# MLA attention one head at a time, with values and ones as the stationary operand of the value products

## The chip, the cores and the metric
One NeuronCore of a Trainium2 chip runs the whole kernel in one launch. The metric is the device time of that core in microseconds (us). Each core has TensorE (PE, matrix products; the loads of its stationary operand are listed as PEld), VectorE (DVE), ScalarE (ACT), GpSimd (POOL) and SyncE (SP, which issues most DMAs). The engines run their own instruction streams in order and wait for each other through semaphores.

## The reference
Two layers of a streaming encoder run for a prompt of 512 new frames and a sample of 32 new frames with 256 cached ones; both share the weights. The part that matters here is branch B of the token mixer, multi-head latent attention (MLA) with 8 heads, keys of 96 features and values of 64:

```python
def attend_mla(q, q_pos, k, v, k_pos):
    s = jnp.einsum('bqhd,bkhd->bhqk', q, k).astype(jnp.float32) * (MLA_QK ** -0.5)
    mask = (k_pos[None, :] // CHUNK) <= (q_pos[:, None] // CHUNK)
    s = jnp.where(mask[None, None], s, -jnp.inf)
    w = jax.nn.softmax(s, axis=-1).astype(v.dtype)
    return jnp.einsum('bhqk,bkhd->bqhd', w, v)
```

CHUNK is 64, so a tile of 128 queries sees all keys up to its own end, and its first 64 queries don't see the last 64 keys. The output of the 8 heads (512 features for each frame) is multiplied by w_br_mla and merged with the two other branches under sigmoid gates.

## The kernel before, in words
In each of the two layers the work comes in stages: entry and projections, keys and queries (kq), stick-breaking attention (the L941 to L971 products), MLA attention, the gated branch products (the loop `branches`), the output projection, the routing and the experts. All MLA operands are f32.

The 544 frames are five tiles: t = 0 to 3 are 128 prompt frames each, t = 4 is the 32 sample frames. MLA runs 40 units, a unit being one tile of queries and one head. `MLA_ORDER = [3, 2, 1, 0, 4]` (L65) puts all 8 heads of tile 3 first (512 keys), then those of tile 2 (384), 1 (256), 0 (128), and the sample's 8 units last (288 keys). For unit n:
- PE `scores(n)`: queries stationary, 128*(t+1) keys moving, into PSUM bank n % 3; for the prompt a one-row product (L1006) adds the mask.
- DVE `neg_max(n)`: the negated maximum of each query's row.
- ACT L1480: the exponential out of PSUM into `pr`, with that maximum as bias; `accum_out` gives the row's sum in `sums` (a second instruction in the trace).
- PE `turn(n)`: transposes of the weights, 128 keys at a time, into bank 3 or 4.
- DVE L1858: copy of the turned weights into `pt` (two buffers).
- PE `values(n)`: for each 128 keys the turned weights [128 keys x 128 queries] are stationary and 64 value columns of the head move; the output [queries x 64] of all heads of the tile lies side by side in bank 5 or 6.

When a tile's 8 heads are done, DVE `normalise` takes the reciprocals of the sums and multiplies the 512 columns, PE `turn_out` (L1051) transposes them in four pieces into bank 7, and ACT `out_rows` (L1472) copies them into `ybr`, which has features on partitions.

PE's order is written out by hand: scores(n+2), values(n-1), turn(n), and two units after a tile's end its turn_out. So the scores run two units ahead. ACT and DVE also split f32 operands of the branch stage into a rounded high part and a low remainder: `high(j)` on ACT (L1443) and `low(j)` on DVE after units 5, 10, 14, 18 and 22, a gate weight after unit 26 (`gate_high`, `gate_low`, 1024 columns), and the remaining eight after the stage. Behind the last unit PE issues filler products, `busy(0, 1)` (L760; the identity times 512 constant columns, read by nobody), turns the last output, and waits for ACT's copy (semaphore o_ev) before `branches`. GpSimd has no part in the stage. `x_ybr[:, 2:6]`, where MLA's output goes, is unused until then; `vv` holds the values of 7 key tiles, 512 columns each. In the kq stage a DVE copy (L1789) fills `vv` for each key tile.

## Time and profile before

| | us |
|---|---|
| median of 3 runs | 1545.51 |
| lowest and highest | 1540.42 and 1546.64 |
| the profiled execution's own time | 1546.93 |
| its span in the trace | 1545.2 |
| mean granted TensorE clock | 0.958 |
| PE busy | 1418.6 (92%) |
| DVE busy | 766.5 (50%) |
| ACT busy | 623.4 (40%) |
| MLA stage, layer 0, first scores to first branch product | 225.06 to 299.21 |

Times inside the trace count from the start of the span. A busy time counts instructions of that engine, and matmuls overlap in it, so that the start of the next instruction says more of a matmul's cost than its length. PEclk is the granted TensorE clock as a share of the full 2.4 GHz.

### The profile page before, as it was taken

The page shows a single profiled execution, that of the slowest core. Times are in us where ns is not written, and L with a number is a line of the kernel's source. Part 1 is how long each engine was busy: PE and PEld are TensorE (multiplying, and loading weights), DVE is VectorE, ACT ScalarE, POOL GpSimd, SP SyncE. Part 2 cuts the span into 40 slices and gives each one's busy share as a digit, 9 for nine tenths or more (in the row PEclk, how much of TensorE's full clock was granted, in tenths as well). Part 3 has the DMA queues.
Part 4 walks back from the last instruction along what each step waited for, and adds up shares of the span by engine and source line. Part 5 has one row for each costly group of instructions (what it writes and reads, how often), then busy time and mean ns, then how long its engine had stood idle before and what let it go on. Part 6 is the DMA issues. An engine that isn't in the chain of part 4 may idle for free.

```text
span 1545.2 us, 21380 instructions
## 1 busy us (share of the span) xinstructions
PE 1418.6 (92%) x8610; PEld 1142.6 (74%) x8610; DVE 766.5 (50%) x1121; ACT 623.4 (40%) x966; POOL 111.2 (7%) x128
## 2 busy tenths in 40 slices
PE   5998999999999988999479999999999999899991
PEld 5995657699999756777279846577999988567760
DVE  4326316534335346887353282265433353578863
ACT  4317634422224144656243285244222241456550
POOL 0300010000000011000203001000000000110002
PEclk9999899899999999999879998998999999999996
DMA  7222300032224456998722102000332263589955
GB/s 259 69 73 97 109 0 1 1 110 71 64 82 172 197 209 236 400 413 309 243 105 69 60 12 98 0 1 1 109 102 68 76 227 127 208 332 418 409 201 201
DMA packets 95928, 229.52 MB, mean 149 GB/s; under 512 B 14410, under 2 KB 64612, under 8 KB 82916
## 3 DMA queue, kind: packets, MB, share of 16 engines
q1 hardware_dynamic: 83252, 179.58, 32.1%
q0 software_dynamic: 7360, 29.89, 5.5%
q10 hardware_dynamic: 5232, 18.88, 3.0%
q8 instruction: 58, 0.95, 0.2%
q14 instruction: 26, 0.21, 0.0%
HBM read 197.69 MB, written 34.84 MB: 150 GB/s over the span
## 4 chain that ended last, share of the span: by engine, by line
PE 86%; DMA 4%; DVE 4%; ACT 3%; issue 2%; POOL 1%; ACTq 0%; POOLq 0%; SPq 0%; DVEq 0%
PE ps L775 10%; PE ps L777 9%; PE ps L776 9%; PE ps L1215 7%; PE ps L1195 3%; PE ps L1194 3%; PE ps L1193 3%; PE ps L941 3%; PE ps L1036 3%; PE ps L801 2%; PE ps L1101 2%; PE ps L1103 2%; PE ps L1102 2%; PE ps L803 2%; PE ps L802 2%; PE ps L760 2%
## 5 line engine op out<-in xcount | busy, mean ns | idle before, releaser
L1672 DVE TENSOR_TENSOR work<-work,ps 128x544 f32<-128x544 f32 x48 | 34.6, 721 | 213.0 <-ACT work L1526 213.0
L1526 ACT ACTIVATE work<-ps 128x544 f32<-128x544 f32 x48 | 30.0, 625 | 249.0 <-PE ps L777 249.0
L776 PE MATMUL ps<-xn_r,ksv_r 128*128 128x272 f32 x384 | 112.9, 294 | 0.0
L776 PE MATMUL ps<-xn_r,work_r 128*128 128x272 f32 x384 | 110.7, 288 | 0.0
L720 POOL DMA_INDIRECT rows_back<-xrow_d,row_of x32 | 38.2, 1193 | 951.5 <-DVE row_of L2001 735.2
L1195 PE MATMUL ps<-ew_r,rows_tok_r 128*128 128x512 f32 x256 | 100.1, 391 | 0.0
L802 PE MATMUL ps<-wr_r,qt_ht_r 128*128 128x256 f32 (+1 forms) x320 | 93.4, 292 | 0.0
L801 PE MATMUL ps<-work_r,qt_ht_r 128*128 128x256 f32 x240 | 72.8, 303 | 14.0 <-DVE rows_lo_r L1672 7.9
L1672 DVE TENSOR_TENSOR ew_r<-ew,gu_hi_a_r 128x2048 fp32r<-128x2048 f32 x32 | 73.1, 2291 | 17.1 <-ACT gu_hi_a_r L1547 17.1
L776 PEld LDWEIGHTS ps<-xn_r,ksv_r 128*128 128x128 f32 x384 | 74.4, 194 | 0.0
L776 PEld LDWEIGHTS ps<-xn_r,work_r 128*128 128x128 f32 x384 | 72.1, 188 | 0.0
L803 PE MATMUL ps<-work_r,rows_lo_r 128*128 128x256 f32 x240 | 71.5, 298 | 0.0
L1480 ACT ACTIVATE work<-ps,nmax 128x512 f32<-128x512 f32 (+4 forms) x80 | 41.6, 519 | 60.0 <-DVE nmax L1837 59.8
L802 PEld LDWEIGHTS ps<-wr_r,qt_ht_r 128*128 128x128 f32 x320 | 65.1, 204 | 0.0
L1837 DVE TENSOR_REDUCE nmax<-ps 128x1 f32<-128x512 f32 (+4 forms) x80 | 38.4, 480 | 53.1 <-PE ps L1006 46.4
L1547 ACT ACTIVATE gu_hi_a_r<-ew 128x2048 fp32r<-128x2048 f32 x32 | 60.7, 1908 | 5.9 <-ACT yo_b L1587 5.9
L760 PE MATMUL ps<-con 128*128 128x512 f32 x92 | 59.3, 782 | 4.0 <-ACT work L1461 4.0
L1102 PE MATMUL ps<-wr_r,qt_ht_r 128*128 128x512 f32 (+1 forms) x160 | 62.7, 392 | 0.0
L801 PEld LDWEIGHTS ps<-work_r,qt_ht_r 128*128 128x128 f32 x240 | 49.9, 208 | 15.4 <-DVE rows_lo_r L1672 9.0
L1672 DVE TENSOR_TENSOR wr_r<-wr,work_r 128x2048 fp32r<-128x2048 f32 x10 | 25.7, 2572 | 70.0 <-ACT work_r L1300 70.0
L1215 PE MATMUL ps<-ew,acts 128*128 128x512 f32 x128 | 58.8, 602 | 1.1 <-issue 1.1
L1215 PE MATMUL ps<-ew,act_b 128*128 128x512 f32 x128 | 57.7, 594 | 1.1 <-issue 1.1
(344 smaller groups left out, 4047.8 us busy)
## 6 DMA issues: line engine op xcount, KB each, us to landing
wr<-in_w_in SPq DMA_DIRECT2D x68, 512.0 KB, 4.7
ew<-in_w_exp_gate SPq DMA_DIRECT2D x32, 1024.0 KB, 7.1
ew<-in_w_exp_up SPq DMA_DIRECT2D x32, 1024.0 KB, 10.8
ew<-in_w_exp_down SPq DMA_DIRECT2D x32, 1024.0 KB, 9.9
wr<-in_w_out SPq DMA_DIRECT2D x16, 512.0 KB, 4.3
rows_d<-yo_a ACTq DMA_DIRECT2D x16, 512.0 KB, 8.2
rows_d<-yo_b ACTq DMA_DIRECT2D x16, 512.0 KB, 8.4
xres_d<-x_keep SPq DMA_DIRECT2D x2, 2048.0 KB, 7.0
```

Source lines behind the costliest of these rows:

```text
L760: mm(bank(b), ident, con[:, 0:512], start=True, stop=True, skip_group_check=True)
L775: mm(out_[h], w_hi, x_hi[:, c], start=first, stop=False, skip_group_check=True)
L776: mm(out_[h], w_hi, x_lo[:, c], start=False, stop=False, skip_group_check=True)
L777: ins = mm(out_[h], w_lo, x_hi[:, c], start=False, stop=last, skip_group_check=True)
L801: mm(bank(g % 6, n), hi_, w_hi[:, k, :], start=(k == 0), stop=False)
L802: mm(bank(g % 6, n), hi_, w_lo[:, k, :], start=False, stop=False)
L803: ins = mm(bank(g % 6, n), lo_, w_hi[:, k, :], start=False, stop=(k == DC - 1))
L1102: mm(bank(b, 512, TM[t]), hi_, wo_low[h][k], start=False, stop=False, skip_group_check=True)
L1195: ins = mm(bank(2 + s), xg_hi[s][:, k, :], low, start=False, stop=(k == DC - 1))
L1215: ins = mm(bank(4 + 2 * s + a), ehT[s][:, P * k:P * k + P], down_w[i][:, k, 512 * a:512 * a + 512], start=(k == 0), stop=(k == 1))
L1547: f(gu_high[s][h], gu_w[i][:, :, 4 * h:4 * h + 4, :].rearrange("p m k n -> p k m n"), ACT.Copy).then_inc(gu_up[0], 1)
L1672: return v_.tensor_tensor(o_, a, b, op)
```

## The change
The units are put in another order (MLA_UNITS): first the sample's 8 heads, then for each head its prompt tiles 3, 2, 1, 0. The value product is turned round: the stationary side is [128 keys x 128 columns], 64 value columns of the head beside 64 ones, and the moving side is up to 512 queries of turned weights. Its output has 64 partitions of features and 64 partitions that all hold the sum of the weights. A head's prompt tiles are collected in `pt` (now two buffers of 4 key blocks x 512 queries), and `values(h)` runs four products for the whole head, of 512, 384, 256 and 128 columns, into bank 6 or 7. The sample's outputs go to bank 5 (`sample_values`).

The values are laid out in groups of 192 columns (even head, ones, odd head). The 7 key tiles don't fit in `vv` like this, so a part of them goes to x_ybr[:, 2:6], and GpSimd writes the ones in the kq stage. ACT's exponentials lose `accum_out`. ACT takes over the copy of tile 3's turned weights (`weights_out`) and computes reciprocals of the denominators as exp(-ln(sum)) over 512 columns on 64 partitions (`denominators`); DVE multiplies (`normalise`) straight into `ybr`. The transposes of the output, `turn_out`, and ACT's `out_rows` are gone. `busy(0, 1)` becomes `busy(0, 2)`.

```diff
@@ -62,14 +62,14 @@
 SBC = 1376
 NEG = -1e30
-MLA_ORDER = [3, 2, 1, 0, 4]
+MLA_UNITS = [(h, 4) for h in range(HEADS)] + [(h, t) for h in range(HEADS) for t in (3, 2, 1, 0)]
...
         aa = work[:, 2 * SBC:4 * SBC].rearrange("p (s n) -> p s n", s=2)
         pr = work[:, 0:1536].rearrange("p (s n) -> p s n", s=3)
-        pt = work[:, 1536:2560].rearrange("p (s n) -> p s n", s=2)
-        ot = work[:, 2560:3072]
+        pt = work[:, 1536:5632].rearrange("p (s j n) -> p s j n", s=2, j=4)
+        pt_s = work[:, 5632:5824].rearrange("p (s n) -> p s n", s=2)
+        rden = work[:, 5824:6336]
...
                  + [big_r[:, (8 + i) * T:(9 + i) * T] for i in range(4)])
+        vv_a, vv_b = vv[:, :, :].rearrange("p t n -> p (t n)"), x_ybr[:, 2:6, :].rearrange("p k n -> p (k n)")
+        VP = 192
+        vv_pairs = [vv_a[:, 4 * VP * j:4 * VP * j + 4 * VP] for j in range(4)] + [None] + [vv_b[:, 4 * VP * j:4 * VP * j + 4 * VP] for j in range(2)]
+        vv_split = [vv_a[:, 16 * VP:18 * VP], vv_b[:, 8 * VP:10 * VP]]
+        def thirds(ap):
...
-        pt_ev = sem("pt_ev", NU)
-        pv_mm = sem("pv_mm", NU)
-        o_nrm = sem("o_nrm", NTILE)
-        o_tr = sem("o_tr", NTILE)
-        o_ev = sem("o_ev", NTILE)
+        pt_ev = sem("pt_ev", NU - HEADS)
+        pt_act = sem("pt_act", HEADS)
+        pv_mm = sem("pv_mm", 2 * HEADS)
+        o_nrm = sem("o_nrm", HEADS + 1)
+        den = sem("den", 2 * HEADS + 4)
         pw_high = sem("pw_high", 6)
         pw_low = sem("pw_low", 6)
...
                     nc.gpsimd.tensor_tensor(xn[:, k, :], f32(rows_hi[:, k, :]), f32(rows_lo[:, k, :]), ALU.add).then_inc(xn_rdy[0], 1)
+                pool.wait_ge(cm_mm[0], at(cm_mm, l, 4))
+                pool.wait_ge(spill[0], at(spill, l, 16))
+                pool.wait_ge(xn_rdy[0], at(xn_rdy, l, DC))
+                stand(pool)
+                for rows_ in (vv_a[:, 0:18 * VP], vv_b[:, 0:10 * VP]):
+                    nc.gpsimd.memset(thirds(rows_)[:, :, 1, :], 1.0).then_inc(ones_in[0], 1)
                 if l == 0:
-                    pool.wait_ge(cm_mm[0], 4)
...
-                    t, h = MLA_ORDER[n // HEADS], n % HEADS
+                    h, t = MLA_UNITS[n]
                     if n >= 3:
                         pe.wait_ge(s_exp[0], at(s_exp, l, n - 2))
...
                 def turn(n):
-                    t = MLA_ORDER[n // HEADS]
+                    t = MLA_UNITS[n][1]
                     pe.wait_ge(s_exp[0], at(s_exp, l, n + 1))
-                    if n >= 2:
-                        pe.wait_ge(pt_ev[0], at(pt_ev, l, n - 1))
+                    if n >= 2 and MLA_UNITS[n - 2][1] == 3:
+                        pe.wait_ge(pt_act[0], at(pt_act, l, MLA_UNITS[n - 2][0] + 1))
+                    elif n >= 2:
...
-                def values(n):
-                    t, h = MLA_ORDER[n // HEADS], n % HEADS
-                    pe.wait_ge(pt_ev[0], at(pt_ev, l, n + 1))
-                    i = n // HEADS
-                    if h == 0 and i >= 2:
-                        pe.wait_ge(o_nrm[0], at(o_nrm, l, i - 1))
-                    dst = ps[0:TM[t], 5 + i % 2, 64 * h:64 * h + 64]
-                    if t < 4:
-                        for j in range(t + 1):
-                            ins = mm(dst, pt[:, n % 2, P * j:P * j + P], vv[:, j, 64 * h:64 * h + 64], start=(j == 0), stop=(j == t))
+                def key_rows(j, h, m=P):
+                    pair, lo = h // 2, VD * (h % 2)
+                    if j == 4:
+                        rows_ = vv_split[pair // 2][0:m, VP * (pair % 2):VP * (pair % 2) + VP]
                     else:
-                        for j in (1, 2):
-                            mm(dst, pt[:, n % 2, DEC * j:DEC * j + DEC], vv[:, 4 + j, 64 * h:64 * h + 64], start=(j == 1), stop=False)
-                        ins = mm(dst, pt[0:DEC, n % 2, 0:DEC], vv[0:DEC, 4, 64 * h:64 * h + 64], start=False, stop=True)
+                        rows_ = vv_pairs[j][0:m, VP * pair:VP * pair + VP]
+                    return rows_[:, lo:lo + P]
+                def sample_values(h):
+                    pe.wait_ge(pt_ev[0], at(pt_ev, l, h + 1))
+                    dst = bank(5, DEC, P, DEC * h)
+                    for j in (1, 2):
+                        mm(dst, key_rows(4 + j, h), pt_s[:, h % 2, DEC * j:DEC * j + DEC], start=(j == 1), stop=False, skip_group_check=True)
+                    ins = mm(dst, key_rows(4, h, DEC), pt_s[0:DEC, h % 2, 0:DEC], start=False, stop=True, skip_group_check=True)
                     ins.then_inc(pv_mm[0], 1)
-                def turn_out(i):
-                    t = MLA_ORDER[i]
-                    pe.wait_ge(o_nrm[0], at(o_nrm, l, i + 1))
-                    if i:
-                        pe.wait_ge(o_ev[0], at(o_ev, l, i))
-                    if t == 4:
-                        stand(pe)
+                def values(h):
+                    pe.wait_ge(pt_ev[0], at(pt_ev, l, HEADS + 3 * h + 3))
+                    pe.wait_ge(pt_act[0], at(pt_act, l, h + 1))
+                    if h >= 2:
+                        pe.wait_ge(o_nrm[0], at(o_nrm, l, h))
                     for j in range(4):
-                        ins = nc.tensor.transpose(bank(7, TM[t], P, P * j), ot[0:TM[t], P * j:P * j + P], ident[0:TM[t], 0:TM[t]])
-                    ins.then_inc(o_tr[0], 1)
+                        ins = mm(bank(6 + h % 2, SEQ - P * j, P, P * j), key_rows(j, h), pt[:, h % 2, j, P * j:SEQ], start=(j == 0), stop=(j == 3), skip_group_check=True)
+                    ins.then_inc(pv_mm[0], 1)
+                pe.wait_ge(ones_in[0], at(ones_in, l, 2))
                 scores(0)
                 scores(1)
                 for n in range(NU):
                     if n + 2 < NU:
                         scores(n + 2)
-                    if n >= 1:
-                        values(n - 1)
+                    if 1 <= n <= HEADS:
+                        sample_values(n - 1)
+                    if n > HEADS and n % 4 == 0:
+                        values(n // 4 - 3)
                     turn(n)
-                    if n % HEADS == 2 and n > HEADS:
-                        turn_out(n // HEADS - 1)
-                values(NU - 1)
-                pe.wait_ge(s_exp[0], at(s_exp, l, NU))
-                busy(0, 1)
-                turn_out(NTILE - 1)
-                pe.wait_ge(o_ev[0], at(o_ev, l, NTILE))
+                values(HEADS - 1)
+                busy(0, 2)
+                pe.wait_ge(o_nrm[0], at(o_nrm, l, HEADS + 1))
                 stand(pe)
                 def branches(dp):
...
-                def out_rows(i):
-                    t = MLA_ORDER[i]
-                    act.wait_ge(o_tr[0], at(o_tr, l, i + 1))
-                    f(ybr[:, 2:6, TO[t]:TO[t] + TM[t]], ps[:, 7, :].rearrange("p (k n) -> p k n", k=4)[:, :, 0:TM[t]], ACT.Copy).then_inc(o_ev[0], 1)
+                def denominators(h):
+                    act.wait_ge(pv_mm[0], at(pv_mm, l, HEADS + h + 1))
+                    if h >= 2:
+                        act.wait_ge(o_nrm[0], at(o_nrm, l, h))
+                    if h >= 0:
+                        q, d = 64 * (h % 2), 64 - 64 * (h % 2)
+                        f(rden[q:q + 64], ps[d:d + 64, 6 + h % 2, :], ACT.Ln).then_inc(den[0], 1)
+                        act.wait_ge(den[0], at(den, l, 2 * h + 5))
+                        f(rden[q:q + 64], rden[q:q + 64], ACT.Exp, scale=-1.0).then_inc(den[0], 1)
+                    else:
+                        for q in (0, 64):
+                            f(rden_s[q:q + 64], out_s[64 - q:128 - q, q // 64:HEADS:2, :], ACT.Ln).then_inc(den[0], 1)
+                        act.wait_ge(den[0], at(den, l, 2))
+                        for q in (0, 64):
+                            f(rden_s[q:q + 64], rden_s[q:q + 64], ACT.Exp, scale=-1.0).then_inc(den[0], 1)
+                def weights_out(n):
+                    h, t = MLA_UNITS[n]
+                    act.wait_ge(pt_mm[0], at(pt_mm, l, n + 1))
+                    if h >= 2:
+                        act.wait_ge(pv_mm[0], at(pv_mm, l, HEADS + h - 1))
+                    f(pt[:, h % 2, 0:t + 1, P * t:P * t + P], ps[:, 3 + n % 2, :].rearrange("p (j n) -> p j n", j=4)[:, 0:t + 1, :], ACT.Copy).then_inc(pt_act[0], 1)
                 for n in range(NU):
-                    t, h = MLA_ORDER[n // HEADS], n % HEADS
+                    h, t = MLA_UNITS[n]
                     m, nk = TM[t], (P * (t + 1) if t < 4 else 288)
                     act.wait_ge(s_max[0], at(s_max, l, n + 1))
                     if n >= 3:
                         act.wait_ge(pt_mm[0], at(pt_mm, l, n - 2))
-                    f(pr[0:m, n % 3, 0:nk], ps[0:m, n % 3, 0:nk], ACT.Exp, bias=nmax[0:m, n % 3:n % 3 + 1],
-                      accum_out=sums[0:m, t, h:h + 1]).then_inc(s_exp[0], 1)
-                    if n % HEADS == 3 and n > HEADS:
-                        out_rows(n // HEADS - 1)
+                    f(pr[0:m, n % 3, 0:nk], ps[0:m, n % 3, 0:nk], ACT.Exp, bias=nmax[0:m, n % 3:n % 3 + 1]).then_inc(s_exp[0], 1)
+                    if n and MLA_UNITS[n - 1][1] == 3:
+                        weights_out(n - 1)
+                    if n >= HEADS and n % 4 == 1:
+                        denominators(n // 4 - 3)
                     if n == 5:
                         act.wait_ge(sv_ev[0], at(sv_ev, l, 4))
...
                         gate_high(0, 0, 0)
-                out_rows(NTILE - 1)
+                denominators(HEADS - 1)
                 for j in range(8, 16):
                     if j == 12:
-                        act.wait_ge(o_ev[0], at(o_ev, l, NTILE))
+                        act.wait_ge(o_nrm[0], at(o_nrm, l, HEADS + 1))
                     high(j)
                 act.preload_act_table_set(TABLE_SIGMOID)
...
                         m = KM[n]
-                        v_.tensor_copy(vv[0:m, n, :].rearrange("p (h n) -> p h n", h=HEADS),
-                                       ps[0:m, b:b + 2, :].rearrange("p b (h n) -> p (b h) n", h=4)[:, :, NOPE:P])
+                        vals = ps[0:m, b:b + 2, :].rearrange("p b (h n) -> p (b h) n", h=4)[:, :, NOPE:P].rearrange("p (q a) n -> p q a n", a=2)
+                        if n == 4:
+                            for i in range(2):
+                                v_.tensor_copy(thirds(vv_split[i])[0:m, :, 0:3:2, :], vals[:, 2 * i:2 * i + 2])
+                        else:
+                            v_.tensor_copy(thirds(vv_pairs[n])[0:m, :, 0:3:2, :], vals)
                         v_.tensor_copy(k3[0:m, :, NOPE:QK], krt[0:m, n, :].unsqueeze(1).to_broadcast([m, HEADS, ROPE])).then_inc(kq_raw[0], 1)
                     else:
...
                     if n >= 3:
                         dve.wait_ge(s_exp[0], at(s_exp, l, n - 2))
                     v_.tensor_reduce(nmax[0:m, n % 3:n % 3 + 1], ps[0:m, n % 3, 0:nk], AX, ALU.max, negate=True).then_inc(s_max[0], 1)
-                def normalise(i):
-                    t, m = MLA_ORDER[i], TM[MLA_ORDER[i]]
-                    dve.wait_ge(pv_mm[0], at(pv_mm, l, HEADS * (i + 1)))
-                    link(v_.reciprocal(sums[0:m, t, :], sums[0:m, t, :]))
-                    if i:
-                        dve.wait_ge(o_tr[0], at(o_tr, l, i))
-                    tt(ot[0:m, :].rearrange("p (h n) -> p h n", h=HEADS), ps[0:m, 5 + i % 2, :].rearrange("p (h n) -> p h n", h=HEADS),
-                       sums[0:m, t, :].unsqueeze(2).to_broadcast([m, HEADS, VD]), ALU.mult).then_inc(o_nrm[0], 1)
+                def normalise(h):
+                    dve.wait_ge(den[0], at(den, l, 2 * h + 6))
+                    if h >= 0:
+                        q = 64 * (h % 2)
+                        tt(ybr[q:q + 64, 2 + h // 2, 0:SEQ], ps[q:q + 64, 6 + h % 2, :], rden[q:q + 64], ALU.mult).then_inc(o_nrm[0], 1)
+                    else:
+                        for q in (0, 64):
+                            ins = tt(ybr[q:q + 64, 2:6, SEQ:T], out_s[q:q + 64, q // 64:HEADS:2, :], rden_s[q:q + 64], ALU.mult)
+                        ins.then_inc(o_nrm[0], 1)
                 neg_max(0)
                 neg_max(1)
                 for n in range(NU):
-                    t = MLA_ORDER[n // HEADS]
+                    t = MLA_UNITS[n][1]
                     if n + 2 < NU:
                         neg_max(n + 2)
-                    dve.wait_ge(pt_mm[0], at(pt_mm, l, n + 1))
-                    if n >= 2:
-                        dve.wait_ge(pv_mm[0], at(pv_mm, l, n - 1))
-                    if t < 4:
-                        v_.tensor_copy(pt[:, n % 2, 0:P * (t + 1)], ps[:, 3 + n % 2, 0:P * (t + 1)]).then_inc(pt_ev[0], 1)
-                    else:
-                        v_.tensor_copy(pt[:, n % 2, DEC:3 * DEC], ps[:, 3 + n % 2, DEC:3 * DEC])
-                        v_.tensor_copy(pt[0:DEC, n % 2, 0:DEC], ps[0:DEC, 3 + n % 2, 0:DEC]).then_inc(pt_ev[0], 1)
-                    if n % HEADS == 1 and n > HEADS:
-                        normalise(n // HEADS - 1)
+                    if t != 3:
+                        dve.wait_ge(pt_mm[0], at(pt_mm, l, n + 1))
+                    h = MLA_UNITS[n][0]
+                    if t == 4:
+                        if h >= 2:
+                            dve.wait_ge(pv_mm[0], at(pv_mm, l, h - 1))
+                        v_.tensor_copy(pt_s[:, h % 2, DEC:3 * DEC], ps[:, 3 + n % 2, DEC:3 * DEC])
+                        v_.tensor_copy(pt_s[0:DEC, h % 2, 0:DEC], ps[0:DEC, 3 + n % 2, 0:DEC]).then_inc(pt_ev[0], 1)
+                    elif t < 3:
+                        if h >= 2:
+                            dve.wait_ge(pv_mm[0], at(pv_mm, l, HEADS + h - 1))
+                        v_.tensor_copy(pt[:, h % 2, 0:t + 1, P * t:P * t + P], ps[:, 3 + n % 2, :].rearrange("p (j n) -> p j n", j=4)[:, 0:t + 1, :]).then_inc(pt_ev[0], 1)
+                    if n >= HEADS and n % 4 == 2:
+                        normalise(n // 4 - 3)
                     if n in (5, 10, 14, 18, 22):
                         low(3 + (5, 10, 14, 18, 22).index(n))
                     if n == 26:
                         dve.wait_ge(g_hi[0], at(g_hi, l, 1))
                         gate_low(0, 0, 0)
-                normalise(NTILE - 1)
+                normalise(HEADS - 1)
                 for j in range(8, 16):
                     low(j)
```

## Rows read from the trace of the kernel before

**Rows 1.** Page, part 4: the chain that ended last, shares by engine.
```profile
PE 86%; DMA 4%; DVE 4%; ACT 3%; issue 2%; POOL 1%; ACTq 0%; POOLq 0%; SPq 0%; DVEq 0%
```
**Rows 2.** Windows around the stage's end; the number before the last two is PEclk.
```profile
286.00:290.00 4.00, 4.00 (x33) 2.34 (x33) 2.60 (x11) 2.03 (x7) 0.00 (x0) 1.00 0.01 2
...
294.00:298.00 4.00, 3.60 (x15) 1.54 (x15) 1.18 (x4) 0.00 (x0) 0.00 (x0) 0.55 0.00 0
298.00:302.00 4.00, 3.19 (x16) 3.06 (x16) 2.71 (x5) 3.56 (x8) 0.00 (x0) 0.50 0.02 4
302.00:306.00 4.00, 4.00 (x24) 4.00 (x23) 3.10 (x6) 3.73 (x5) 0.00 (x0) 0.67 0.00 0
```
**Rows 3.** Timeline of PE, one unit of 512 keys: start, length, instruction.
```profile
231.58 1.02 PE L1004 MATMUL ps<-big,qt_ht 96*128 96x512 f32 x2
232.54 0.20 PE L1006 MATMUL ps<-negrow,halfrow 1*128 1x64 bf16 x1
232.67 1.10 PE L1036 MATMUL ps<-vv,work 128*128 128x64 f32 x8
233.61 0.61 PE L1020 MATMUL ps<-con,work 128*128 128x128 f32 x4
234.05 1.02 PE L1004 MATMUL ps<-big,qt_ht 96*128 96x512 f32 x2
```
**Rows 4.** Timeline of PE, one unit of 256 keys.
```profile
264.56 0.66 PE L1036 MATMUL ps<-vv,work 128*128 128x64 f32 x4
265.06 0.39 PE L1020 MATMUL ps<-con,work 128*128 128x128 f32 x2
265.28 0.60 PE L1004 MATMUL ps<-big,qt_ht 96*128 96x256 f32 x2
265.81 0.20 PE L1006 MATMUL ps<-negrow,halfrow 1*128 1x64 bf16 x1
```
**Rows 5.** Timeline of PE, one unit of the sample request.
```profile
289.14 0.67 PE L1008 MATMUL ps<-big,qt_ht 96*32 96x288 f32 x2
289.65 0.39 PE L1039 MATMUL ps<-vv,work 128*32 128x64 f32 x4
...
290.20 0.30 PE L1023 MATMUL ps<-con,work 32*128 32x32 f32 x2
...
290.46 0.67 PE L1008 MATMUL ps<-big,qt_ht 96*32 96x288 f32 x2
```
**Rows 6.** Timeline of PE: a turn of the output, and the stage's end.
```profile
277.87 0.66 PE L1051 MATMUL ps<-con,work 128*128 128x128 f32 x4 [0.28 <-DVE work L1672]
...
294.85 0.63 PE L1039 MATMUL ps<-vv,work 128*32 128x64 f32 x4 [0.40 <-DVE work L1861]
...
295.77 2.08 PE L760 MATMUL ps<-con 128*128 128x512 f32 x2
297.77 0.63 PE L1051 MATMUL ps<-con,work 32*128 32x32 f32 x4
299.21 0.59 PE L775 MATMUL ps<-lT_r,ksv_r 128*128 128x272 f32 x1 [0.81 <-ACT x_ybr L1472]
```
**Rows 7.** Groups on DVE, 225 to 300 us: busy us, mean ns, idle before.
```profile
L1837 DVE TENSOR_REDUCE nmax<-ps 128x1 f32<-128x512 f32 x8 | 5.5, 692 | 22.5 <-PE ps L1006 22.5
L1837 DVE TENSOR_REDUCE nmax<-ps 128x1 f32<-128x256 f32 x8 | 3.4, 422 | 0.4
L1672 DVE TENSOR_TENSOR work<-ps,sums 128x512 f32<-128x512 f32 x4 | 2.8, 691 | 0.1
L1672 DVE TENSOR_TENSOR ksv_r<-wr,ksv_r 128x1024 fp32r<-128x1024 f32 x1 | 1.2, 1212 | 0.0
```
**Rows 8.** Groups on ACT, 225 to 300 us.
```profile
L1480 ACT ACTIVATE work<-ps,nmax 128x256 f32<-128x256 f32 x8 | 3.8, 474 | 5.3 <-DVE nmax L1837 5.3
L1472 ACT ACTIVATE x_ybr<-ps 128x512 f32<-128x512 f32 x4 | 2.4, 598 | 7.3 <-PE ps L1051 7.3
L1443 ACT ACTIVATE kst_r<-x_ybr 128x544 fp32r<-128x544 f32 x2 | 1.3, 644 | 0.0
```
**Rows 9.** Timeline of ACT after the last turn.
```profile
298.44 0.28 ACT L1472 ACTIVATE x_ybr<-ps 128x128 f32<-128x128 f32 x1 [6.20 <-PE ps L1051]
```

13 lines of the change are left out of this document (9 added, 4 removed).

## The prediction

> **What bounds the kernel now.** I read the chain of waits first, then the windows, then the timeline of PE in the MLA stage, then the groups of DVE and ACT. The chain is 86% PE and 4% DVE [rows 1], so a stage is worth what PE spends in it. MLA takes 225.06 to 299.21 us in layer 0, 74.15 us, and repeats in layer 1. Within a prompt unit one PE instruction starts when the one before ends, with no wait marked [rows 3, 4]: copies, maxima and exponentials are hidden. Only the end differs. The last values waited 0.40 us for a copy, filler products follow, and the branch products start after a wait of 0.81 us for ACT [rows 6]. There the granted clock fell to 0.55 and 0.50, that is to the 1.2 GHz level, and was full again only inside the window 302:306; it was 1.00 in the dense sample units before [rows 2].
>
> **PE's prices.** From starts, not lengths. A score product costs 0.96 us for 512 keys and 0.53 for 256 [rows 3, 4], so 0.106 plus 0.213 for each 128 moving columns: 0.75 and 0.32 for 384 and 128. The mask adds 0.13 [rows 3]. A turn costs 0.11 for each 128 keys [rows 3, 4]. Old values cost 0.94 for four key blocks and 0.50 for two [rows 3, 4], so about 0.72 and 0.28 between and below: 2.44 us a head.
>
> **The wide value products.** The trace has no such product. The score row is the nearest (f32, 128 stationary columns, up to 512 moving): 0.96 + 0.75 + 0.53 + 0.32 = 2.56 us a head, or 0.12 more than now, 1 us a layer. Half the price, 1.28, is the lower end, if columns of a full 128-row product streamed faster; no row shows that. 2.8 is the upper end. I take 2.56: the new form moves twice the columns in a fifth of the products, and the two effects cancel.
>
> The Trainium skill, page "TensorE: Matmul & The Clock Gate", section "Part 2: What happens when you issue a matmul", says that the next tile's weights load while this tile's matmul runs. The fixed 0.106 us of every product would then vanish for wide ones: 10 x 0.213 = 2.13 us a head, 3.4 us a layer less. The score rows keep the 0.106 at 512 columns, where there is most time to hide it, so I give the rule a chance as a rival and not the sum.
>
> **What goes.** Four turns of the output inside the stage, about 0.45 each plus one wait of 0.28 [rows 6], some 2.1 us. The row-sum instruction on ACT goes from every exponential and shortens nothing on PE, as the exponential isn't late now. In the new order it helps, and I count exponentials at their own length.
>
> **The new order, one head.** The values of head h stand ahead of the turn of the next head's tile 3. I count from their start. PE: values to 2.56, turn of 4 blocks to 3.0, scores of tile 0 to 3.45, turn of 3 to 3.8, scores of the following head's tile 3 to 4.9, then the turn of tile 1 is due. It needs that tile's exponential, and on ACT this now stands behind three instructions that did not exist there: the copy of the turned tile 3 (0.60), the Ln of the denominators from PSUM (0.60) and their Exp (0.63, from the 0.64 of 544 columns) [rows 8]. The copy can start when the turn has drained, at 3.2. On one engine the next instruction starts 0.09 before the length of the one before is over; a hand-over costs 0.04 (298.40 to 298.44) [rows 6, 9]. So Ln starts at 3.7, Exp at 4.35, the exponential of tile 1 (0.47) at 4.9, and PE turns at 5.4: a wait of 0.53. PE goes on with 0.22 + 0.88 + 0.11 + 0.66 and wants the next head's values at 7.26. DVE by then: copy of tile 1 from 5.8 (0.42), normalise (0.69), maximum of 384 keys (0.56, between 0.69 and 0.42), copy of tile 0 (0.29), each 0.09 overlapped [rows 7]. That ends at 7.5, a second wait of 0.29. The period is 7.54 us, of which 6.7 is PE's work; half a head on PE is no longer cover for the copies and exponentials, since the values no longer lie between the turns.
>
> The operand splits after n = 10, 14, 18 and 22 all fall on tile 1, that is between normalise and the copy that the values wait for. Each adds 0.62 (0.72 for 544 columns, between the 0.69 and 1.21 of rows 7, less overlap). The gate weight at n = 26 adds 1.13 [rows 7]. In the old order the same instructions lay in units whose copy wasn't late.
>
> **The stage.** (1) Sample units with the first head's scores, up to the first wide values: 15 score products 9.8, turns 3.2, sample values 8 x 0.50 (now 0.55; fewer columns move, wider loads) [rows 5], and waits of 0.2 + 0.3 + 0.7: 18.2. (2) Three periods with a split, 3 x 8.16 = 24.5. (3) One with the gate weight, 8.67. (4) Two plain, 15.1. (5) The last head has no scores to put between: from the sixth head's follow-on at 3.8 PE waits 1.62 for the turn of tile 1, then 0.05, then 1.30 for the last copy: 7.07. (6) Last values 2.56, drain 0.17 (the four transposes at 233.61 take 0.61 and the next product starts after 0.44 [rows 3]), Ln 0.60, Exp 0.63, multiply 0.69, four hand-overs 0.16, and 0.49 from ACT's end at 298.72 to the first branch product [rows 6, 9]: 5.3. The filler of 1.9 lies beside this chain. Sum 78.8. The same way of adding gives 68.8 us to the old kernel's last value product, which started at 69.8, so I add 1.0: 79.8 us against 74.15, at a full clock.
>
> **The clock.** The old stage's low clock cost the branch products 1.4 us up to 302 and 1.3 after it, 2.7 in all [rows 2]; so old stage and cost are 76.85. In the new one PE waits 2.9 of 3.3 us right before the last values. The old fall came behind three waits of 0.40, so I expect one here too, but with 4.5 us of dense products behind it: the last values run mostly at the 1.2 GHz level, +2.0, and 0.2 of the rest. Bounds are 0 and the 5.1 that the old windows lost. 79.8 + 2.2 = 82.0.
>
> **Elsewhere.** In the kq stage the copy of key tile 4 is split in two, +0.15 us on DVE. GpSimd's ones are written before that stage, where POOL and DVE idle; if this cover failed, PE's first scores would wait by the two memsets, a few us. DVE's new wait for the spill is one that ACT has already passed.
>
> **Sum.** 82.0 + 0.15 - 76.85 = 5.3 us a layer, 10.6 for two. Against the profiled execution's 1546.93 (span 1545.2) that is 1557.5; that execution lies 1.4 above the median shown, so 1556 is forecast.
>
> **Rivals.**
> - *The clock holds at the end.* The waits are short enough or the dense part saves it: 2.2 a layer less, +6.2 in all, 1552. For it: one value stretch and filler of 4.5 us follow. Against it: the old fall came with shorter waits.
> - *Loads hide.* The page's rule above: 3.4 a layer less than the forecast, +3.8, 1549. Against it: rows 3 and 4.
> - *The sample units cost the clock as well.* They now stand together at the start with still fewer moving columns. If the clock falls there, 2.7 us a layer more as in the old branch start, 1561. Against it: PEclk 1.00 in 286:290 [rows 2].
> - *Slack, the other side.* On busy time alone ACT has 4.0 and DVE 3.9 of the 6.7 us of a head, and PE waited nearly nowhere in the old stage. If my waits don't arise (copies and exponentials run ahead as before), up to 12 us of waits a layer vanish: 79.8 - 12 + 0.15 - 76.85 = -9, 1528. It decides from the point where less than 5 of the 12 us are left: then the kernel is faster by over 0.5%. Against it: Ln and Exp can't start before the values and the turn ahead of them in PE's order, whatever the loads.
> - *The change doesn't do what it says*, as when a wait for GpSimd's ones holds the stage: the trace gives no reason for one, and it lies within the forecast's spread.
>
> **How the numbers follow.** Forecast 0.42, clock holds 0.22, loads hide 0.12, sample units slow too 0.12, slack 0.12. Half a per cent is 7.7 us, about what a measurement of this kernel can tell from no change; slower begins at 1553.2. Of the forecast's own spread (1551 to 1561) a quarter lies below that. Slower: 0.31 + 0.05 + 0.12 + 0.02 = 0.50. Faster: the slack case, 0.12. Same: 0.38. The range leaves out the slack case and little above: from 1545, which takes in loads hidden with the clock held, to 1567, which takes in the low clock at both ends and Ln and Exp at 0.7 us (+1.4 a layer).
>
> **What would show it.** PE in the MLA stage of the changed kernel: value products of 2.5 to 2.6 us a head, starting 8.1 us apart for the first heads and 7.5 for the later ones. A wait of about 0.5 for ACT ahead of each turn of tile 1, and one of 0.3 (0.9 with a split) for DVE ahead of the values. A wait of over 1 us twice ahead of the last values, and PEclk at 0.5 behind them. No L1051 rows, no row-sum instructions. First branch product near 307 us in layer 0. I am wrong on the order if the period is near 6.7, on the products if their rows cost under 2.2 a head, on the clock if PEclk is 1.00 from the last values on.

## The result, and the profile after

The changed kernel takes 1595.11 us (median of 5 executions, 1586.18 to 1597.64) against 1545.51 for the kernel before: a ratio of 1.0308, 95% interval [1.0274, 1.0343]. It is slower by some 48 us, where 1556 had been forecast and 1567 was the upper end of the range. The profiled execution is the quickest of the five (its own time 1586.18, span 1584.4). Its MLA stage (first scores to first branch product) lasts 223.83 to 323.25 us in layer 0, 99.42 us against 74.15, and 99.43 in layer 1. So the two stages alone give 50.6 us, while the whole span is only 39.2 us longer: outside the stages this execution is 11 us shorter than the one profiled before. About 5.4 of these are the 2.7 us a layer that the prediction counted for the old kernel's low clock behind the stage, since the branch products now start at full clock (1.00 in 322:326, against 0.50 and 0.67 in [rows 2]). For the rest the mean granted clocks of the two traces give an estimate. The changed kernel lost 0.055 of 1584.4, 87 us, of which 37.5 lie in the stages and the first branch products; the kernel before lost 0.042 of 1545.2, 65 us, of which 10.2 lie there. So elsewhere this execution lost some 5 us less. The other four executions are 9 to 11 us longer, at a mean granted clock of 0.937 to 0.940.

The chain of waits, shares by engine, against [rows 1]; PE's share is smaller, since more of the span is spent waiting:
```profile
PE 82%; DVE 5%; ACT 4%; DMA 4%; issue 4%; POOL 1%; ACTq 0%; POOLq 0%; SPq 0%; DVEq 0%
```
Windows through the stage, layer 0. After the bounds come the length, then busy time (and count) of PE, PEld, DVE, ACT, POOL, then PEclk, DMA share and GB/s:
```profile
226.00:230.00 4.00, 4.00 (x23) 2.56 (x23) 1.82 (x8) 1.47 (x3) 0.00 (x0) 0.84 0.00 0
230.00:250.00 20.00, 20.00 (x72) 13.16 (x70) 5.19 (x17) 3.43 (x7) 0.00 (x0) 0.50 0.01 1
250.00:254.00 4.00, 4.00 (x14) 1.78 (x12) 1.84 (x5) 3.16 (x9) 0.00 (x0) 0.67 0.00 0
262.00:306.00 44.00, 35.59 (x159) 20.37 (x159) 23.09 (x48) 23.02 (x43) 0.00 (x0) 1.00 0.00 1
...
314.00:318.00 4.00, 2.78 (x6) 1.35 (x7) 1.30 (x3) 0.21 (x1) 0.00 (x0) 0.51 0.01 2
318.00:322.00 4.00, 4.00 (x11) 2.48 (x9) 0.00 (x0) 1.18 (x2) 0.00 (x0) 0.64 0.00 0
322.00:326.00 4.00, 3.34 (x24) 2.75 (x23) 3.90 (x7) 3.98 (x9) 0.00 (x0) 1.00 0.00 0
```
Two different losses can be read here. From 230 to 250 PE is busy for every one of 20 us, and runs at half its clock. From 262 to 306 the clock is full and PE is idle for 8.4 of 44 us. The first costs up to 10 us in these windows, so the two are of one size, and only experiments can say what each is worth.

PE's timeline in the sample units (start, length, instruction), against [rows 5]:
```profile
226.49 0.63 PE L1059 MATMUL ps<-work,x_ybr 128*128 128x32 f32 x4
227.05 0.40 PE L1060 MATMUL ps<-work,vv 32*128 32x32 f32 x2
227.30 0.29 PE L1042 MATMUL ps<-con,work 32*128 32x32 f32 x2
...
229.53 1.17 PE L1025 MATMUL ps<-big,qt_ht 96*32 96x288 f32 x2
230.63 1.06 PE L1059 MATMUL ps<-work,x_ybr 128*128 128x32 f32 x4
...
232.46 1.17 PE L1025 MATMUL ps<-big,qt_ht 96*32 96x288 f32 x2
```
None of these is marked with a wait; the last wait ahead of them is one of 0.18 us at 225.66. The value products of one sample unit take 0.81 us at full clock (226.49 to 227.30), against 0.55 before. A whole unit takes 1.65 us at full clock (225.89 to 227.54) and 2.93 at the low level (229.53 to 232.46), against 1.32 before at full clock. The clock falls at 228.7 and is full again from 252.6. The last value product of the sample ends at about 248.7, so the low level lasts 4 us into the first head's prompt units.

PE's timeline in one head and at the stage's end, against [rows 3, 6]:
```profile
265.92 2.42 PE L1069 MATMUL ps<-work,vv 128*128 128x512 f32 x8 [0.80 <-DVE work L1907]
268.18 0.60 PE L1039 MATMUL ps<-con,work 128*128 128x128 f32 x4
...
271.24 0.44 PE L1039 MATMUL ps<-con,work 128*128 128x128 f32 x2 [0.64 <-ACT work L1515]
...
274.46 2.42 PE L1069 MATMUL ps<-work,vv 128*128 128x512 f32 x8 [1.18 <-DVE work L1907]
...
314.00 0.90 PE L1039 MATMUL ps<-con,work 128*128 128x128 f32 x3 [1.64 <-ACT work L1515]
316.12 4.63 PE L1069 MATMUL ps<-work,vv 128*128 128x512 f32 x8 [1.21 <-DVE work L1907]
320.54 2.05 PE L777 MATMUL ps<-con 128*128 128x512 f32 x4
323.25 0.39 PE L792 MATMUL ps<-lT_r,ksv_r 128*128 128x272 f32 x1 [0.66 <-DVE x_ybr L1708]
```
And what PE waited for in the stage (us in total, times, longest):
```profile
PE ps L1069 <- DVE work L1907: 7.4, 8, 1.6
PE ps L1039 <- ACT work L1515: 5.5, 7, 1.6
```
The wide values take 2.26 us (265.92 to 268.18), 3.95 where the clock is mostly low (306.99 to 310.94). They start at 256.13, 265.92, 274.46, 282.63, 291.67, 299.20, 306.99 and 316.12.

### The profile page after: what moved, and what is told of

Read it like the earlier page. It is cut to its first block, busy times and chain, and to the rows that moved or that the text cites. A ratio compares the mean times of both kernels' runs of the same rounds, so it can differ in the third digit from the quotient of the medians.

```text
span 1584.4 us, 20880 instructions
## 1 busy us (share of the span) xinstructions
PE 1440.0 (91%) x8382; PEld 1142.5 (72%) x8382; DVE 758.9 (48%) x1107; ACT 640.4 (40%) x932; POOL 112.6 (7%) x132
## 4 chain that ended last, share of the span: by engine, by line
PE 82%; DVE 5%; ACT 4%; DMA 4%; issue 4%; POOL 1%; ACTq 0%; POOLq 0%; SPq 0%; DVEq 0%
PE ps L792 9%; PE ps L794 9%; PE ps L793 9%; PE ps L1230 7%; PE ps L1208 3%; PE ps L1209 3%; PE ps L1210 3%; PE ps L1069 3%; PE ps L958 3%; PE ps L1116 2%; PE ps L1118 2%; PE ps L1117 2%; PE ps L818 2%; PE ps L820 2%; PE ps L819 2%
## 5 line engine op out<-in xcount | busy, mean ns | idle before, releaser
L1878 DVE TENSOR_REDUCE nmax<-ps 128x1 f32<-128x512 f32 (+2 forms) x80 | 38.3, 479 | 110.5 <-PE ps L1023 67.5
L1069 PE MATMUL ps<-work,vv 128*128 128x512 f32 (+3 forms) x128 | 49.8, 543 | 14.8 <-DVE work L1907 14.8
L1515 ACT ACTIVATE work<-ps,nmax 128x512 f32<-128x512 f32 (+2 forms) x80 | 39.7, 519 | 53.7 <-DVE nmax L1878 53.3
L777 PE MATMUL ps<-con 128*128 128x512 f32 x96 | 56.1, 719 | 4.0 <-ACT work L1476 4.0
```

The lines of the kernel that those rows point to most:

```text
L1069: ins = mm(bank(6 + h % 2, SEQ - P * j, P, P * j), key_rows(j, h), pt[:, h % 2, j, P * j:SEQ], start=(j == 0), stop=(j == 3), skip_group_c ...
```

## Experiments

Each time is a median. The ratio beside it is to the kernel before, run in the same session, with its 95% interval in brackets; "stage" is the time from the first scores to the first branch product, of layer 0 where one number stands.

Two causes compete for the loss. One: the sample's products, with 32 moving columns and now at the front of the stage, bring the clock down though PE never waits. The other: the waits of the heads, for ACT's exponential and DVE's copy, are the loss, and the clock falls behind waits only.

**Fillers in the sample units.** The changed kernel with one 512-column filler product after each sample turn:
```diff
                     turn(n)
+                    if n < HEADS:
+                        busy(7, 1)
```


> The changed kernel with one filler product of 512 columns behind the turn of each of the 8 sample units (bank 7, read by nobody). Theory, the thin sample units standing together cost the clock: PEclk stays at 1.00 over them, a sample unit takes 1.65 + 0.96 = 2.6 us instead of the 2.9 at the low level, the first wide values start 28.3 us after the stage's start (32.3 in the changed kernel) and run at the full level (2.3 us, not 3.9), some 5.5 us a layer less: ratio to the kernel before about 1.024. Rival, the clock falls for the waits at the stage's start and not for the thin units: the fall stays and the fillers only add, 1.035 or more. Rival, the new order's waits in the heads are nearly all of the loss: 1.03, no change.

1581.11 us, ratio 1.0249 [1.02, 1.0299]. Stage 95.6 us.
```profile
224.00:252.00 28.00, 26.41 (x127) 14.89 (x127) 10.96 (x33) 8.47 (x18) 0.00 (x0) 1.00 0.00 1
...
282.00:306.00 24.00, 20.56 (x82) 12.29 (x82) 10.27 (x22) 9.26 (x18) 0.00 (x0) 0.86 0.00 1
```
The clock now holds over the sample units, so they are where it fell. But the fillers (1.06 us each) eat most of what they give back: wide values begin 30.2 us in (28.3 expected, 32.3 without fillers), the stage is 3.8 us shorter (5.5 expected), and the clock now falls among the heads, from 283 to 290 and 310 to 314. The ratio came out as expected.

**Denominators and normalising later.** They move from the second and third tile of a head to the fourth, so that neither stands ahead of tile 1's exponential nor ahead of tile 0's copy:
```diff
-                    if n >= HEADS and n % 4 == 1:
+                    if n >= HEADS and n % 4 == 3:
                         denominators(n // 4 - 3)
...
-                    if n >= HEADS and n % 4 == 2:
+                    if n >= HEADS and n % 4 == 3:
                         normalise(n // 4 - 3)
```

> The changed kernel with the denominators (Ln, Exp on ACT) and normalise (DVE) of a head moved from behind the exponential of tile 2 and the copy of tile 1 to behind those of tile 0. Theory, each head waits on PE for the exponential of tile 1 behind them (0.64) and for the copy ahead of the values: the 0.64 goes in 7 heads, the 1.64 at the end too, about half of the waits ahead of the values stays where an operand split stands there: 6 to 8 us a layer less, ratio about 1.022. The fall of the clock in the sample units stays. Rival, the clock alone makes the loss: 1.03.

1557.43 us, ratio 1.0085 [1.0061, 1.011]. Stage 86.9 and 84.1 us. All waits behind the first scores sum to 4.1 us in layer 0 and 4.5 in layer 1, against 13.7 in both.
```profile
224.00:260.00 36.00, 35.82 (x138) 21.74 (x136) 12.84 (x39) 10.73 (x23) 0.00 (x0) 0.62 0.00 1
262.00:282.00 20.00, 18.43 (x86) 11.00 (x85) 11.56 (x26) 11.29 (x22) 0.00 (x0) 1.00 0.00 1
```
This gives 34 us by the ratios, far more than I expected; the stages of the two profiled executions account for 28 of them. The waits it removes are some 9 us a layer; the rest in the stages is clock that falls less among the heads, once in layer 0 (285 to 289) and not at all in layer 1. The front is nearly as slow as it was: wide values begin 30.9 us in, and the clock is low for 28 us (230 to 258) where it was low for 24.

**The old kernel with its sample tile first.** One line of the kernel before:
```diff
-MLA_ORDER = [3, 2, 1, 0, 4]
+MLA_ORDER = [4, 3, 2, 1, 0]
```

> The kernel before with MLA_ORDER = [4, 3, 2, 1, 0]: its own narrow products, the sample's 8 units first. Theory A, any 8 sample units in a row behind the stick-breaking stage cost the clock: PEclk 0.5 from the fourth or so, 5 to 8 us a layer more at the start, 3 to 5 given back at the end, ratio 1.00 to 1.01. Theory B, it is the new form of the sample's value products (wide stationary side, 32 moving columns, 1.65 us a unit instead of 1.31) that makes them thin: PEclk stays 1.00 at the start, and the stage ends with tile 0 at the full clock, ratio 0.993 to 0.998.

1545.99 us, ratio 0.9994 [0.996, 1.0027].
```profile
222.00:240.00 18.00, 17.72 (x119) 9.44 (x116) 11.09 (x33) 8.68 (x26) 0.00 (x0) 1.00 0.01 1
...
282.00:306.00 24.00, 21.15 (x122) 17.50 (x120) 12.77 (x29) 10.82 (x27) 0.00 (x0) 0.79 0.00 1
```
Sample units in a row at the front don't lower the clock in their old form. So the place alone isn't the cause, and the form remains, which the last two runs test. The time fits neither expectation well: theory B wanted 0.993 to 0.998 and full clock at the stage's end, but PE now waits for copies in tile 0 (0.38 us three times) and the clock is low from 291 to 301, as long as at the end of the kernel before.

**Both mended, with fillers.** The changed kernel with the fillers and the late denominators above, and the operand splits of ACT and DVE moved off tile 1:
```diff
-                    if n in (5, 10, 14, 18, 22):
-                        high(3 + (5, 10, 14, 18, 22).index(n))
-                    if n == 26:
+                    if n in (5, 11, 15, 19, 23):
+                        high(3 + (5, 11, 15, 19, 23).index(n))
+                    if n == 27:
```

> Fillers of the first, late denominators of the second, and the operand splits moved from units 10, 14, 18, 22 and 26 to 11, 15, 19, 23 and 27, behind normalise. Theory: the gains add, 5.5 for the clock, 6 to 8 for the waits, 2 for the splits, 14 to 16 us a layer, ratio 1.010 to 1.013. Rival, with fewer waits PE runs into the next engine (DVE) at once: 1.02.

1550.74 us, ratio 1.0041 [1.0016, 1.0065]. This is better than the 1.010 to 1.013 expected. Stage 78.7 us in both layers, full clock throughout, wide values 6.68 us apart (the last pair 5.12), that is PE's own work without a wait. What remains is the fillers, 8.5 us a layer, and the dearer sample products.

**Half the stationary width.** The sample's value products hold only the 64 ones in the array instead of 128 columns; the sample's MLA output is left out:
```diff
-                        mm(dst, key_rows(4 + j, h), pt_s[:, h % 2, DEC * j:DEC * j + DEC], start=(j == 1), stop=False, skip_group_check=True)
+                        mm(dst, key_rows(4 + j, h)[:, one], pt_s[:, h % 2, DEC * j:DEC * j + DEC], start=(j == 1), stop=False, skip_group_check=True)
...
```


> The changed kernel; the sample's value products keep only the 64 columns of ones on the stationary side, so the sample's own output of MLA is left out. Theory, it is the 128-column load in front of 32 moving columns that makes a sample unit 1.65 us instead of 1.31: the six value instructions take 0.5 us instead of 0.81, a unit 1.35. If a shorter unit is also dense enough, PEclk stays 1.00 and the first wide values start 20 to 22 us after the stage's start (32.3 in the changed kernel). Rival, the moving side of 32 columns alone is what the clock falls for: the fall stays, some 29 us.

1578.83 us in one execution. Two rows of PE's timeline, and a window:
```profile
227.01 0.42 PE L1060 MATMUL ps<-work,x_ybr 128*64 128x32 f32 x4
227.36 0.30 PE L1061 MATMUL ps<-work,vv 32*64 32x32 f32 x2
```
```profile
225.00:255.00 30.00, 30.00 (x117) 16.04 (x116) 11.21 (x36) 9.03 (x20) 0.00 (x0) 0.54 0.00 1
```
From start to start the two products over full key blocks (four instructions) take 0.35 us where with 128 stationary columns they took 0.56: the width of the stationary side sets most of their price. A unit takes 1.45 us at full clock (1.35 expected) against 1.65. Halving the width did not hold the clock, which fell as before (low from 227.8 to 254.5).

**Sample units between prompt units.** Late denominators and moved splits; the sample's units alternate with those of the first two heads, no fillers:
```diff
+SAMPLE_HEADS = [4, 5, 6, 7, 0, 1, 2, 3]
+PROMPT_HEADS = [7, 6, 5, 4, 3, 2, 1, 0]
+PROMPT_UNITS = [(h, t) for h in PROMPT_HEADS for t in (3, 2, 1, 0)]
+MLA_UNITS = [u for i in range(8) for u in ((SAMPLE_HEADS[i], 4), PROMPT_UNITS[i])] + PROMPT_UNITS[8:]
```


> The same late order, no fillers, and the sample's units laid one by one between the units of the first two heads, so that no stretch is thin (heads in the order 7 to 0, sample heads 4 to 7, 0 to 3, since outputs overwrite the values held in x_ybr). Theory: PEclk 1.00 through the stage, no 7.6 us of fillers: stage 71 to 72 us instead of 78.7 and of the old 74.15 plus the 2.7 that its low clock costs behind it: ratio 0.990 to 0.994. Rival, ACT and DVE can't keep two kinds of unit apart by two steps only and PE waits: 75 us or more, ratio 0.997 or more.

1558.0 us, ratio 1.0087 [1.0061, 1.0114], stage 84.9.
```profile
224.00:266.00 42.00, 40.66 (x157) 23.11 (x156) 15.57 (x44) 12.97 (x25) 0.00 (x0) 0.72 0.00 1
```
The expectation (1.00 throughout, 0.990 to 0.994) failed. The clock is low from 234 to 245 and again from 251 to 265. Mixing the units makes two low stretches of one, 24 us together against 31 in the next run, and doesn't remove them.

**The same without mixing or fillers.** The kernel of the fourth experiment without its fillers:
```diff
-                    if n < HEADS:
-                        busy(7, 1)
```

> Late denominators and splits as in the combined kernel, without the fillers. Theory, two falls are at work and independent of each other: the one in the sample units comes back (first wide values 31 to 32 us after the start instead of 28.6), the heads stay at the full clock, 6.7 us apart: 3 us a layer more than the combined kernel, ratio 1.008. Rival, with the fillers' 7.6 us gone it is as fast as the combined kernel or faster.

1557.85 us, ratio 1.0066 [1.004, 1.0092], stage 84.2 and 82.8.
```profile
224.00:262.00 38.00, 37.04 (x136) 22.38 (x135) 12.62 (x38) 10.81 (x23) 0.00 (x0) 0.60 0.00 1
262.00:282.00 20.00, 19.93 (x92) 11.59 (x91) 12.84 (x27) 12.46 (x24) 0.00 (x0) 1.00 0.00 1
```
The expected 1.008 lies inside the interval. The heads run at full clock and nearly without waits, and the front alone is left: low from 230 to 261, though the last value product of the sample ends at about 250.7. So the low level can outlast them by 10 us of dense prompt products.

**Fillers at the old kernel's end.** In the kernel before, one filler product after each of the last three turns:
```diff
                     turn(n)
+                    if n >= NU - 3:
+                        busy(n % 3, 1)
```

> The kernel before with one filler product of 512 columns behind the turn of each of its last three units, where PE waited 0.40 for the copy. Theory, the waits in thin units let the clock fall at the old stage's end: with fillers PEclk stays 1.00 up to the branch products, 2 us of filler beyond the waits against 4 to 5 us of low clock, ratio 0.996 to 0.998. Rival, the clock falls in spite of them: 1.002.

1540.99 us, ratio 0.9962 [0.9937, 0.9987].
```profile
285.00:300.00 15.00, 14.16 (x98) 8.83 (x97) 7.25 (x21) 6.99 (x18) 0.00 (x0) 1.00 0.01 1
```
The stage is 0.3 us longer (74.47) and the branch products start at full clock, where it was 0.50 before [rows 2]. By the ratio the gain is 2.9 us a layer (1.0 to 4.9), so the low clock behind the stage did cost about the 2.7 that the prediction charged for it.

**The sample's value products in their old form.** Now the disputed part by itself, with everything else of the change left in. The transposed weights stand in the array and 64 value columns move; the sample's sums come from its exponentials again, with one reciprocal, one multiply and four small transposes:
```diff
-                    dst = bank(5, DEC, P, DEC * h)
+                    dst, val = ps[0:DEC, 5, 64 * h:64 * h + 64], slice(VD * (h % 2), VD * (h % 2) + VD)
                     for j in (1, 2):
-                        mm(dst, key_rows(4 + j, h), pt_s[:, h % 2, DEC * j:DEC * j + DEC], start=(j == 1), stop=False, skip_group_check=True)
+                        mm(dst, pt_s[:, h % 2, DEC * j:DEC * j + DEC], key_rows(4 + j, h)[:, val], start=(j == 1), stop=False)
...
+                      **({"accum_out": sums[0:m, h:h + 1]} if t == 4 else {})).then_inc(s_exp[0], 1)
...
+                        link(v_.reciprocal(sums[0:DEC, :], sums[0:DEC, :]))
...
+                            ins = nc.tensor.transpose(bank(5, DEC, P, P * j), ot[0:DEC, P * j:P * j + P], ident[0:DEC, 0:DEC])
...
```
Once on the changed kernel as it is:

> The same old form of the sample's value products, with everything else of the change as it stands (denominators at the second tile, normalising at the third, splits at their old units). Theory A: the clock holds over the sample units, wide values begin 18 to 20 us after the first scores instead of 32.3; the waits of the heads (about 10 us) and the clock falls among them stay: stage 84 to 87 us against 99.4, ratio 1.011 to 1.017. Rival (the heads' waits alone would bring the clock down as much once the front no longer does): low stretches in the heads grow to 20 us or more, stage over 90 us, ratio above 1.020.

1562.37 us, ratio 1.012 [1.0103, 1.0136]. Stage 86.82 us in layer 0, wide values begin 19.6 us in instead of 32.3.
```profile
222.60:242.60 20.00, 19.04 (x124) 10.43 (x125) 12.68 (x38) 9.59 (x26) 0.00 (x0) 1.00 0.00 1
262.00:282.00 20.00, 16.54 (x62) 9.55 (x61) 9.15 (x18) 8.90 (x16) 0.00 (x0) 0.84 0.00 0
```
The first expectation holds: full clock at the front, the waits and three short falls among the heads unchanged in kind, 12.6 us a layer gone. Of these some 2.2 are the cheaper value products (0.27 a unit); the rest is clock.

And once on the kernel with late denominators and moved splits, with no fillers but the change's own at the end:

> The sample's value products in their old form (the transposed weights stand in the array, the head's 64 value columns move; sums by the exponentials, one reciprocal and one multiply, four small transposes), everything of the heads as the change has it, denominators and normalising at the fourth tile and the splits at units 5, 11, 15, 19 and 23, no fillers. Theory A (the products with only 32 moving columns bring the clock down in the sample units): granted clock 1.00 over the sample units, unit about 1.3 us instead of 1.65 at full clock and 2.9 at the low level, heads 6.7 us apart as before, stage 69 to 72 us against 83 to 84 without this edit, against 74.2 of the kernel before: time about 1530 to 1538 us, ratio 0.990 to 0.996, below the kernel before. Theory B (any run of sample units at the front brings it down when what lies ahead of it is the new value packing): clock still 0.50 over most of them, stage about 82 us, ratio 1.004 to 1.008.

1528.34 us, ratio 0.9891 [0.9874, 0.9908]: faster than the kernel before by 17 us, the best of all, and a little better than the 0.990 to 0.996 expected. PE's timeline of one sample unit, of the first two wide values and of the end:
```profile
225.57 0.67 PE L1027 MATMUL ps<-big,qt_ht 96*32 96x288 f32 x2
226.08 0.39 PE L1061 MATMUL ps<-x_ybr,work 128*32 128x64 f32 x4
226.40 0.29 PE L1062 MATMUL ps<-vv,work 32*32 32x64 f32 x2
226.62 0.31 PE L1044 MATMUL ps<-con,work 32*128 32x32 f32 x2
...
226.89 0.67 PE L1027 MATMUL ps<-big,qt_ht 96*32 96x288 f32 x2
...
240.46 2.42 PE L1071 MATMUL ps<-work,vv 128*128 128x512 f32 x8
242.72 0.60 PE L1041 MATMUL ps<-con,work 128*128 128x128 f32 x4
...
286.19 2.42 PE L1071 MATMUL ps<-work,vv 128*128 128x512 f32 x8 [0.38 <-DVE work L1915]
...
291.12 0.39 PE L794 MATMUL ps<-lT_r,ksv_r 128*128 128x272 f32 x1 [0.79 <-DVE x_ybr L1715]
```
```profile
222.10:291.10 69.00, 67.11 (x336) 38.19 (x336) 41.17 (x97) 38.90 (x82) 0.00 (x0) 1.00 0.00 1
```
The stage is 69.0 us in both layers at full clock. A sample unit is back at 1.32 us (225.57 to 226.89), its value products at 0.54. Against the seventh experiment, the same order with the new form in the sample (84.2 and 82.8 us), this one edit takes 15.2 and 13.8 us off the stage.

The two repairs add up. By the ratios against 1545 us, the old form of the sample is worth 29 us (1.0308 to 1.012), the later denominators 34 (1.0308 to 1.0085), and both, with the moved splits, 64 (1.0308 to 0.9891).

## Why the prediction was wrong

The sign was right and the kind of every wait; the size was not. The forecast had 78.8 us of steps, 1.0 of correction and 2.2 for the clock, 82.0 in all, for a stage that took 99.4. By its own terms, layer 0:

| step | forecast, full clock | measured |
|---|---|---|
| (1) up to the first wide values | 18.2 | 32.3 |
| (2) to (4) six periods | 48.2 | 50.9 |
| (5) last period | 7.07 | 9.13 |
| (6) last values to first branch product | 5.3 | 7.13 |

- **The clock, the step that failed.** The prediction expected one fall, behind the waits at the end, and gave the sample units a chance of 0.12 with "2.7 us a layer more as in the old branch start". The mechanism of that rival is what happened, and its size was wrong by more than four times. Step (1) took 14.1 us more than forecast: 2.5 are the sample's dearer value products (next point), and the other 11.6 or so, against the rival's 2.7, go with the low clock. The windows bound it: 226 to 254 lose 0.16 x 4 + 0.5 x 20 + 0.33 x 4 = 12.0 us at most, and since a unit's time goes up by 1.78 and not by 2 (2.93 over 1.65), 24 us at the low level come to 10.5. The rival's 2.7 was only the part of the old fall that lay in the branch products; here the new form goes on through the rest of the eight units, and the low level goes on with it and 4 us beyond: 24 us. The row set against it, PEclk 1.00 in the old sample units [rows 2], was a row of products with 64 moving columns and 32 stationary, and the third experiment shows that it stays true of those wherever they stand. It was no evidence on the new form.
- **Sample values at 0.50 a unit.** They measured 0.81 at full clock, 2.5 us a layer more, also a term that failed. "Fewer columns move, wider loads" was named and then booked as a gain, with no row of such a product. The row with half the stationary width (0.35 for two products against 0.56) shows that the loads outweigh the columns. The Trainium skill, page "TensorE: Matmul & The Clock Gate", section "LDWEIGHTS (loading the stationary operand)", says that a load takes its time by the stationary columns and not by the contraction rows. The trace agrees: two products with 128 stationary columns over 128 key rows take 0.56 us (226.49 to 227.05), so 0.28 each, and one over 32 key rows takes 0.25 (227.05 to 227.30). Halving the columns took the 0.56 to 0.35. This rule would have spoken against the change's sample part. With the units in their old form, step (1) measures 19.6 us in the change's order, 0.6 of it a wait for the four small transposes, and 18.4 in the late order, where the waits in the forecast's 18.2 are mostly gone.
- **Wide values at 2.56 a head.** They measure 2.26: 2.4 us a layer less. That is ten times 0.213 and 0.13 once, as if the fixed 0.106 of the score rows were paid about once and not by each of the four products; the trace gives only the sum. The rival "loads hide" had 2.13 and was nearer than the forecast; it gave 2.4 of its 3.4 us a layer and was buried by the rest.
- **The waits.** Forecast about 12 us a layer, measured 12.9. Ahead of tile 1's turn 0.64 (forecast 0.53), ahead of the values 0.16 and 0.43 without a split (0.29), 0.80 and 1.18 with one (0.9), 1.63 with the gate weight (1.4), at the end 1.64 and 1.21 (1.62 and 1.30). At full clock the periods were 8.54 and 8.17 with a split (8.16), 9.04 with the gate weight (8.67), 7.53 and 7.79 plain (7.54). So the slack rival was rightly small for this order of the instructions. But its period, 6.68 us without a wait, is what the kernels with late denominators and moved splits reach: ACT and DVE had the slack that their busy time promised, and the order kept it from being used. The prediction saw the three instructions in the way and didn't ask what moving them would be worth.
- **What the waits cost beyond themselves.** They were priced as idle time. The later denominators removed about 9 us of waits a layer and took 12.5 and 15.3 us off the stages. The difference is clock: among the heads there are falls at 256 to 259.4, 307 to 310.6 and 314 to 321 in the changed kernel, and one short fall in layer 0 of the mended one. The forecast put 2.2 us on the last of these and nothing on the others.
- **What the range missed.** Its upper end allowed the low clock at both ends, at 2.7 and 2.2 us. It bounded the size of a fall by the one fall that the old trace had, not by the length of the stretch that might cause it. At half clock the first term could be 36 us (18.2 doubled, an estimate), and the range should have reached for that if the rival deserved a chance at all.
- **Not shown.** The form of the sample's value products is shown as the cause of the fall at the front, by one edit on two kernels (the row sums and four small transposes that the old form needs come with it). Which feature of it lowers the clock is open: halving the stationary side to 64 columns did not mend it, and going to 64 moving with 32 stationary did, which changes both sides at once. 64 moving beside 128 stationary and 32 moving beside 32 stationary weren't run. Why the low level outlasts the sample by 4 us in one kernel and by 10 in another is open too.

## What to carry to other kernels

Turning a product round is a choice for each size: here it gained for 512 queries (2.44 to 2.26 us a head) and lost for 32 (0.55 to 0.81 a unit), and the best version uses each form where it fits. The new form of the sample's products cost twice, by its loads and by the clock, and the clock's part lasted through them and 4 to 10 us beyond, with hardly a wait on PE. So a possible fall is better priced by the length of the stretch that may cause it than by a fall seen elsewhere. When an order is written by hand, look for what stands ahead of the next engine's input: moving three instructions one or two tiles later was worth 34 us by the ratios.

## What the runs showed of the hardware

- The granted clock went to its lower level (1.2 GHz) in a stretch where PE was busy 20.00 of 20.00 us. The Trainium skill, page "TensorE: Matmul & The Clock Gate", section "Part 1: The HAM clock gate (the "warmup" mystery)", ties the lower level to an idle engine. This trace disagrees: PE is busy for 4.00 of 4.00 us in the window in which the clock falls (226 to 230), and its only waits since the stage began are 0.78 us at its start and 0.18 at 225.66. The busy share counts instructions and doesn't say how much of the array worked.
- With the sample's value products in their old form (64 moving, 32 stationary) the clock stayed at 1.00 over these units at the front of the stage, in three kernels (third experiment and the last two). With 32 moving beside 128 or 64 stationary and no fillers it fell there in all five.
- Filler products of 512 columns between the sample units held the clock at 1.00 over the same units, at 1.06 us each. Prompt units between them did not (0.72 over 224 to 266).
- At the end of the old kernel's stage, three such fillers are worth more than they cost: ratio 0.9962 [0.9937, 0.9987].
- The low level outlasted the last of the sample's value products: by 4 us in the changed kernel (248.7 to 252.6), by 10 in the seventh experiment (250.7 to 260.8).
